# A chunked recurrence of a decoder step: turns of matrices by 64x64 products with the identity instead of 128x128 transposes

## The chip, the core and the metric

The kernel runs on one core of one Trainium2 chip. Its engines work side by side, each through its own list of instructions: TensorE (PE for its products, PEld for the loading of the stationary operand), VectorE (DVE), ScalarE (ACT), GpSimd (POOL) and SyncE (SP, which here only starts DMA transfers). They wait for each other by semaphores. The metric is the device time of one execution in microseconds (us), less is better; the median of three executions counts.

## The reference

One inference step of a two-layer decoder: an RWKV-7 time mix with a mixture of experts, then attention over a shared key/value projection with a second mixture of experts, for a prompt of 512 rows (D = 1024) and 8 single-row requests, all in fp32. The change touches only the recurrence of the time mix. Per head (16 heads of 64 features) and per row t of the prompt it is

```
def step(s, inp):
    r_t, w_t, k_t, v_t, a_t, b_t = inp
    sa = jnp.einsum('bhij,bhj->bhi', s, a_t)
    s = s * w_t[:, :, None, :] + sa[..., None] * b_t[:, :, None, :] + v_t[..., None] * k_t[:, :, None, :]
    return s, jnp.einsum('bhij,bhj->bhi', s, r_t)
s_fin, y = lax.scan(step, s0, xs)
```

with a 64x64 state s per head, started at zero for the prompt. y goes on through a norm, a gate and a projection; s_fin is an output.

## The kernel before, in words

`time_mix_chunks` cuts the 512 rows into 8 chunks of 64 and turns the scan into products. All 16 heads go together: two heads share the 128 partitions (a pair; hp says which half), and four quads of two pairs (q, p2) lie beside each other. Within a chunk the dependence of a row on earlier rows is a triangular 64x64 system per head. Its inverse is built in Tt in 5 levels, by doubling. A level (numbered l) of chunk k is a chain through four steps:

- PE turns Tt to get T (`turn_t`, 4 transposes of 128x128 through the identity, L620), and makes X from N and Tt (`solve_x`, 16 products of 64x64 with 32 columns, L606)
- DVE masks X (L766), ACT copies T out of PSUM (L841, L843)
- PE multiplies T and X (`solve_d`, 16 products, L627)
- DVE subtracts the result from Tt (L772), and the next level can start.

Two other kinds of work are laid between these steps, as fillings. The chunk behind (k-1) gets its state work: `state_v`, `state_m` (L677, L686), `turn_w` (L694), `state_u` (L704), `out_u` (L711), `add_m` (L721), one per level. The chunk ahead (k+1) is prepared: `scores_n`, `scores_b`, `scores_k` (L639, L646, L653) and the turns of V, B and K (`turn_v_b` L659 and L662, `turn_k` L668). The order is written out by hand in the loops over k and l at the end of each engine's block; nothing plans it. k runs from 0 to 8: chunk 0 has no state work beside it, chunk 7 no preparation, and k = 8 is state work alone. Ahead of the loop PE multiplies the identity with constants in `warm` (L591), results unused. POOL scales the operands of coming chunks (L910, L918). SP fills two large DRAM tables (L581, L584) at the beginning.

Of the products, 64x64 ones use one quadrant of the PE array each, by the half of the input partitions and the half of the output partitions; the list `quads` orders them so that neighbours are in other quadrants. An fp32 product stands in the trace as two LDWEIGHTS and two MATMUL records, a transpose as one of each.

Of the kernel before, what the change touches and what calls it, by code (L numbers as in the profile page):

```python
# [30 lines left out]
PAIRS = HEADS // 2  # L31
# [484 lines left out]
def time_mix_chunks(core, f, kk):  # L516
# [10 lines left out]
    with ExitStack() as own:  # L527
# [7 lines left out]
        Bt, Kt = [[by_quad(part(3, 2 * n + i, 512)) for i in range(2)] for n in range(2)]  # L535
# [3 lines left out]
        N, Tt, V, VS = tiles("N", 2, by_head), tiles("Tt", 2, by_quad), tiles("V", 3, by_quad), tiles("VS", 2, by_pair)  # L539
# [11 lines left out]
        v_ready, bt_ready, kt_ready = S("v_ready"), S("bt_ready"), S("kt_ready")  # L551
        v_copied, bt_copied, kt_copied = S("v_copied"), S("bt_copied"), S("kt_copied")
        tt0_first, tt0_new = S("first_tt0"), S("tt0_new")
        x_ready, x_masked, t_turned, t_copied, d_ready, tt_new = S("x_ready"), S("x_masked"), S("t_turned"), S("t_copied"), S("d_ready"), S("tt_new")
# [6 lines left out]
        ident = core.c("ident")  # L561
        over = lambda name, shape: core.c(name).rearrange("p (o t) -> p o t", o=1).to_broadcast([128] + shape)
# [13 lines left out]
        with nc.Block() as block:  # L576
# [11 lines left out]
            def _(pe):  # L588
                def warm(n):
                    for i in range(n):  # L590
                        pe.matmul(ps[i % 2][:, :], ident, core.const[:, 0:512], start=True, stop=True)  # L591
# [3 lines left out]
                def solve_x(k, l):  # L595
                    if l == 1:
                        pe.wait_ge(n_copied, 2 * k + 2)
                        if k:
                            pe.wait_ge(tt0_new, k)
                            pe.wait_ge(tt_new, 10 * k)  # L600
                        else:
                            pe.wait_ge(tt0_first, 1)
                    else:
                        pe.wait_ge(tt_new, 2 * (5 * k + l - 1))
                    for q, p2, hp in quads:
                        ins = pe.matmul(ps[p2][rows[hp], 32 * q:32 * q + 32], N[k % 2][rows[p2], hp, q], blocks(Tt[k % 2][rows[p2], q, hp], l, 1),  # L606
                                        start=True, stop=True)
                    ins.then_inc(x_ready, 1)

                def turn_t(k, l):  # L610
                    if l > 1:
                        pe.wait_ge(tt_new, 2 * (5 * k + l - 1))
                    elif k:
                        pe.wait_ge(tt0_new, k)
                    else:
                        pe.wait_ge(tt0_first, 1)
                    if 5 * k + l > 1:
                        pe.wait_ge(t_copied, 5 * k + l - 1)
                    for q in range(QUADS):
                        ins = pe.transpose(ps[2][:, 128 * q:128 * q + 128], Tt[k % 2][:, q], ident)  # L620
                    ins.then_inc(t_turned, 1)

                def solve_d(k, l):
                    pe.wait_ge(x_masked, 2 * (5 * k + l))
                    pe.wait_ge(t_copied, 5 * k + l)
# [4 lines left out]
                def scores_n(c):  # L630
                    if c:
                        pe.wait_ge(staged, 5 * c)
                        pe.wait_ge(kt_copied, c)
                        pe.wait_ge(bt_copied, c)
                    else:
                        pe.wait_ge(staged_first, 5)
# [19 lines left out]
                def turn_v_b(c):  # L656
                    pe.wait_ge(ks_copied, 2 * c + 2)
                    for q in range(QUADS):
                        ins = pe.transpose(ps[3][:, 128 * q:128 * q + 128], VS[c % 2][:, 2 * q:2 * q + 2], ident)  # L659
                    ins.then_inc(v_ready, 1)  # L660
                    for q in range(QUADS):
                        ins = pe.transpose(ps[4][:, 128 * q:128 * q + 128], B[c % 2][:, 2 * q:2 * q + 2], ident)  # L662
                    ins.then_inc(bt_ready, 1)

                def turn_k(c):
                    pe.wait_ge(v_copied, c + 1)
                    for q in range(QUADS):
                        ins = pe.transpose(ps[3][:, 128 * q:128 * q + 128], K[c % 2][:, 2 * q:2 * q + 2], ident)  # L668
                    ins.then_inc(kt_ready, 1)

                def state_v(c):
                    if c:
                        pe.wait_ge(m_sum, 2 * c)
                    pe.wait_ge(v_copied, c + 1)
# [6 lines left out]
                def state_m(c):  # L681
                    pe.wait_ge(vk_done, c + 1)
                    pe.wait_ge(m_new, c + 1)
                    for q, p2, hp in quads:
                        p = 2 * q + p2
                        ins = pe.matmul(wy[p2][rows[hp], :, q], M[rows[hp], p], AR[c % 4][rows[hp], p], start=False, stop=q == QUADS - 1)  # L686
                    ins.then_inc(wt_ready, 1)

                def turn_w(c):
                    pe.wait_ge(wt_copied, 2 * c + 2)  # L690
                    if c:
                        pe.wait_ge(u_copied, c)
                    for q in range(QUADS):
                        ins = pe.transpose(ps[7][:, 128 * q:128 * q + 128], WT[:, 2 * q:2 * q + 2], ident)  # L694
                    ins.then_inc(w_ready, 1)

                def state_u(c):
                    pe.wait_ge(w_copied, c + 1)
                    pe.wait_ge(tt_new, 10 * c + 10)
                    for q in range(QUADS):  # L700
                        for hp in range(2):
                            for p2 in range(2):
                                at_u = 256 * hp + 64 * q
                                ins = pe.matmul(ps[7][rows[p2], at_u:at_u + 64], Tt[c % 2][rows[p2], q, hp], W[rows[p2], q, hp], start=True, stop=True)  # L704
                    ins.then_inc(u_ready, 1)

                def out_u(c):
                    pe.wait_ge(u_copied, c + 1)
                    pe.wait_ge(y_first, 2 * c + 2)
# [4 lines left out]
                def add_m(c):  # L714
                    pe.wait_ge(y_copied, 2 * c + 2)
                    pe.wait_ge(kt_copied, c + 1)
                    for q in range(QUADS):
                        for i in range(2):
                            for p2, hp in ((0, 0), (1, 1), (0, 1), (1, 0)):
                                left, right = ((Bt[c % 2], U[rows[p2], hp, q]), (Kt[c % 2], V[c % 3][rows[p2], q, hp]))[i]  # L720
# [8 lines left out]
                scores_k(0)  # L729
                turn_v_b(0)  # L730
                for k in range(CHUNKS + 1):
                    chain, state, prep = k < CHUNKS, k >= 1, k + 1 < CHUNKS
                    for l in range(1, 6):
                        if chain:
                            turn_t(k, l)
                            solve_x(k, l)
                        if chain and l == 1:
                            turn_k(k)
# [13 lines left out]
                        if prep and l == 2:  # L752
                            scores_n(k + 1)
                        if prep and l == 3:
                            scores_b(k + 1)
                        if prep and l == 4:
                            scores_k(k + 1)
                        if prep and l == 5:
                            turn_v_b(k + 1)

            @block.vector
            def _(dve):
                def mask(k, l):
                    dve.wait_ge(x_ready, 5 * k + l)
                    for p2 in range(2):
                        dve.tensor_tensor(X[:, p2], piece(p2, 0, 32), over(f"level{l}", [QUADS, 32]), ALU.mult).then_inc(x_masked, 1)  # L766
# [33 lines left out]
                dve.tensor_copy(VS[0], f["v"][:, :, at(0)]).then_inc(staged_first, 1)  # L800
# [6 lines left out]
                for k in range(CHUNKS + 1):  # L807
                    chain, state, prep = k < CHUNKS, k >= 1, k + 1 < CHUNKS
                    for l in range(1, 6):
                        if chain:  # L810
                            mask(k, l)
                        if prep and l == 4:
                            keep_b(k + 1, 1)
                        if prep and l == 5:
                            keep_k(k + 1, 1)
                        if chain:
                            add(k, l)
                        if prep and l == 3:
                            keep_b(k + 1, 0)
                        if prep and l == 4:  # L820
                            keep_k(k + 1, 0)
                        if state and l == 4:
# [5 lines left out]
            def _(act):  # L828
                def exps(c):
                    if c == 2:  # L830
                        act.wait_ge(staged_first, 5)
                    if c > 2:
                        act.wait_ge(staged, 5 * (c - 2))
# [3 lines left out]
                def copy_t(k, l):  # L837
                    act.wait_ge(t_turned, 5 * k + l)
# [1587 lines left out]
```

## Time and profile before

| | us |
|---|---|
| median of three executions (lowest, highest) | 2183.52 (2180.32, 2188.89) |
| the profiled execution, its span | 2186.08, 2184.3 |
| chunk loop, `warm` to last state update | 295.0 to 488.8 |
| TensorE busy over the span | 1641.3 (75%) |
| mean granted clock of TensorE | 0.884 of 2.4 GHz |

The span is from the first to the last instruction of the profiled execution. The profile gives a page of sums, and the trace can be asked for stretches: busy time and counts per engine, instructions in order of time, DMA packets per queue. Times in the rows are from the start of the span. A bracket behind a row is the idle time of that engine ahead of it, with what ended it; "issue" is time in which it waited for nothing that the trace shows.

### The profile page before, as it was taken

The numbers are of one execution on the slowest core, as the hardware profiler recorded it, in microseconds if no ns is written. First come the engines' busy times: TensorE is split into PE (matmuls) and PEld (weight loads), VectorE is DVE, ScalarE is ACT, GpSimd is POOL, SyncE is SP. The second block draws the span as 40 slices with busy tenths as digits, with TensorE's granted clock in tenths as the row PEclk, the third lists the DMA queues.
The fourth block names the chain that finished last, engine by engine and source line by source line (L and its number), as shares of the span: only waits on it lengthen the run. The fifth ranks groups of instructions, "written<-read, shape, count | busy, mean of one in ns | idle before, by whom it ended". The sixth has DMA issues, their size and how long they took to land. (4 is left out here: it accounts for less than half of the span.)

```text
span 2184.3 us, 46140 instructions
## 1 busy us (share of the span) xinstructions
PE 1641.3 (75%) x20476; PEld 1226.1 (56%) x20476; DVE 627.5 (29%) x1584; ACT 374.4 (17%) x885; POOL 180.7 (8%) x166
## 2 busy tenths in 40 slices
PE   2999859981238934999980898999999526999990
PEld 2788738860225722666650676888787323666650
DVE  3100264435452152111117002000661431111117
ACT  0300323321020030111112010001660200111112
POOL 1000023410000022000004000000000120000004
PEclk7999969995578976999995998999999758999995
DMA  6020051001401136999956214442202184999953
GB/s 197 20 77 20 0 235 39 4 4 51 157 25 37 60 123 247 388 386 387 374 184 252 36 39 127 116 120 67 99 2 78 58 295 151 385 383 386 373 203 141
DMA packets 218733, 345.34 MB, mean 158 GB/s; under 512 B 69673, under 2 KB 116433, under 8 KB 218282
## 3 DMA queue, kind: packets, MB, share of 16 engines
q1 hardware_dynamic: 191354, 289.07, 37.5%
q0 software_dynamic: 9856, 33.81, 5.0%
q10 hardware_dynamic: 17328, 19.51, 2.7%
q8 instruction: 164, 2.69, 0.5%
q14 instruction: 31, 0.25, 0.0%
HBM read 295.56 MB, written 46.78 MB: 157 GB/s over the span
## 5 line engine op out<-in xcount | busy, mean ns | idle before, releaser
L1729 PE MATMUL bank<-ring_extra,xT 128*32 128x256 f32 x3456 | 194.4, 379 | 9.0 <-issue 9.0
L2123 PE MATMUL bank<-x,ring 128*128 128x256 f32 (+1 forms) x768 | 174.0, 387 | 3.4 <-issue 2.7
L426 PE MATMUL bank<-mix,ring 128*128 128x260 f32 x768 | 172.8, 386 | 4.3 <-issue 3.1
L1729 PEld LDWEIGHTS bank<-ring_extra,xT 128*32 128x32 f32 x3456 | 133.6, 110 | 65.6 <-issue 17.2
L426 PEld LDWEIGHTS bank<-mix,ring 128*128 128x128 f32 x768 | 146.1, 192 | 31.0 <-issue 8.8
L2123 PEld LDWEIGHTS bank<-x,ring 128*128 128x128 f32 x768 | 146.1, 192 | 28.1 <-issue 5.4
L1729 PE MATMUL bank<-ring,xT 128*32 128x256 f32 x2688 | 155.5, 385 | 7.5 <-issue 6.2
L1521 DVE TENSOR_TENSOR sg<-sg,bank 128x128 f32<-128x128 f32 x96 | 27.3, 285 | 377.7 <-ACT sg L1618 377.7
L1729 PEld LDWEIGHTS bank<-ring,xT 128*32 128x32 f32 x2688 | 101.7, 112 | 56.7 <-issue 15.2
L1818 PE MATMUL bank<-ring,x 128*128 128x256 f32 (+1 forms) x480 | 108.0, 386 | 2.5 <-PEq L2308 1.3
L1818 PEld LDWEIGHTS bank<-ring,x 128*128 128x128 f32 (+1 forms) x480 | 82.3, 173 | 28.3 <-issue 7.4
L1748 PE MATMUL bank<-ring_extra,hT 128*32 128x256 f32 x1728 | 97.0, 380 | 0.0
L1618 ACT ACTIVATE sg<-bank 128x128 f32<-128x128 f32 x96 | 26.7, 278 | 334.6 <-PE bank L1729 334.6
L1748 PE MATMUL bank<-ring,hT 128*32 128x256 f32 x1344 | 75.4, 380 | 0.0
L1748 PEld LDWEIGHTS bank<-ring_extra,hT 128*32 128x32 f32 x1728 | 54.9, 110 | 35.6
L1207 PE MATMUL bank<-ring,x 128*128 128x256 f32 (+1 forms) x320 | 72.1, 386 | 2.1 <-PEq L189 1.5
L1207 PE MATMUL bank<-ring,w 128*128 128x256 f32 (+1 forms) x320 | 72.1, 386 | 1.7 <-PEq L1129 1.1
L1624 ACT ACTIVATE yo<-bank 128x256 f32<-128x256 f32 x96 | 36.9, 384 | 192.9 <-PE bank L1748 192.9
L1207 PEld LDWEIGHTS bank<-ring,x 128*128 128x128 f32 (+1 forms) x320 | 55.0, 174 | 18.9 <-issue 5.0
L1207 PEld LDWEIGHTS bank<-ring,w 128*128 128x128 f32 (+1 forms) x320 | 54.9, 173 | 18.9 <-issue 4.9
L1748 PEld LDWEIGHTS bank<-ring,hT 128*32 128x32 f32 x1344 | 43.3, 110 | 27.2 <-issue 0.2
L1767 POOL DMA_DIRECT2D xe<-expert_in x32 | 16.4, 512 | 505.9 <-PE bank L1670 496.7
(364 smaller groups left out, 2177.8 us busy)
## 6 DMA issues: line engine op xcount, KB each, us to landing
ring_extra<-in_moe_w_gate SPq DMA_DIRECT2D x72, 512.0 KB, 9.5
ring_extra<-in_moe_w_up SPq DMA_DIRECT2D x72, 512.0 KB, 12.9
ring_extra<-in_moe_w_down SPq DMA_DIRECT2D x36, 1024.0 KB, 15.1
ring<-in_moe_w_gate SPq DMA_DIRECT2D x56, 512.0 KB, 9.2
ring<-in_moe_w_up SPq DMA_DIRECT2D x56, 512.0 KB, 12.6
ring<-in_moe_w_down SPq DMA_DIRECT2D x28, 1024.0 KB, 14.5
ring<-in_a_w_rkv SPq DMA_DIRECT2D x12, 1024.0 KB, 5.0
xe<-expert_in POOLq DMA_DIRECT2D x32, 384.0 KB, 8.0
```

The source lines that it names most:

```text
L426: ins = pe.matmul(ps[2 * (job % 4) + h][:, 0:HALF], w[:, kt, q * 128:(q + 1) * 128], m[:, kt, h * HALF:(h + 1) * HALF], start=kt == 0, sto ...
L1207: ins = pe.matmul(ps[job % 8][0:n, 0:256], z[:, kt, t * 128:t * 128 + n], w[:, kt, :], start=kt == 0, stop=kt == KT - 1)
L1521: dve.tensor_tensor(sg[:, u], sg[:, u], ps[i % 2][:, 0:128], ALU.mult).then_inc(gd, 1)
L1618: act.activation(sg[:, u], ps[i % 2][:, 0:128], ACT.Sigmoid).then_inc(sd, 1)
L1624: act.activation(yo[e % 2][:, u], ps[3 + i % 2][:, 0:256], ACT.Copy).then_inc(yc, 1)
L1729: ins = pe.matmul(ps[i % 2][32 * q:32 * q + 32, 0:256], xT[:, kt, 32 * u:32 * u + 32], gate_up(w[kt // 2], kt % 2, q), start=kt == 0, stop ...
L1748: ins = pe.matmul(ps[3 + i % 2][32 * r:32 * r + 32, 0:256], hT[:, u, 32 * k:32 * k + 32], w[k // 2].rearrange("p (k n) -> p k n", k=2)[:, ...
L1767: pool.dma_start(xe[e % 2][0:CAP, :], core.expert_in[CAP * e:CAP * e + CAP, :]).then_inc(xl[e % 2], 16)
L1818: ins = pe.matmul(ps[job % 6][0:n, 0:256], x[:, kt, t * 128:t * 128 + n], w[:, kt, :], start=kt == 0, stop=kt == KT - 1)
L2123: ins = pe.matmul(ps[2 * (job % 3) + h][:, 0:n], w[:, kt_, rr, :], z[:, kt_, lo:lo + n], start=kt_ == 0, stop=kt_ == 7)
```

## The change

- T, V, B, K and W are turned by 64x64 products with the identity, 16 for each matrix, where there were 4 transposes of 128x128 each. `solve_x` and `turn_t` become one function: product X and turn T alternate, 32 products, in two halves with a semaphore each, so that DVE and ACT get the first half earlier. T comes through two banks, and ACT and DVE work by halves.
- V is read from its own place; the copies to VS on DVE (L800) and POOL (L918) go. PSUM bank 7 carries T now, W and U share banks 5 and 6 with the state.
- The order of `state_m` is by pair and head half. `state_u` also waits until ACT has copied y.
- The preparation moves up a level: `scores_n` to level 1, `scores_b` to 2, `scores_k` to 3, `turn_v_b` to 4, `turn_k` to 5 (it was in level 1 of its own chunk). ACT and DVE follow.
- `warm` is called three more times: twice with 3 ahead of the loop, and once with 1 in each level of chunk 0 (its product is 128x512).

```diff
@@ PE @@
-                        pe.matmul(ps[i % 2][:, :], ident, core.const[:, 0:512], start=True, stop=True)
+                        pe.matmul(ps[5 + i % 2][:, :], ident, core.const[:, 0:512], start=True, stop=True)
...
-                def solve_x(k, l):
-                    if l == 1:
+                def solve_x_and_turn_t(k, l):
+                    if l > 1:
+                        pe.wait_ge(tt_new, 2 * (5 * k + l - 1))
...
-                    for q in range(QUADS):
-                        ins = pe.transpose(ps[2][:, 128 * q:128 * q + 128], Tt[k % 2][:, q], ident)
-                    ins.then_inc(t_turned, 1)
+                        pe.wait_ge(t_copied, 2 * (5 * k + l - 1))
+                    w = 64 if l == 1 else 32
+                    for x2 in range(2):
+                        t2 = 1 - x2
+                        right = eye[t2] if l == 1 else blocks(eye[t2], l, 0)
+                        for q in range(QUADS):
+                            for hp in range(2):
+                                x = pe.matmul(ps[x2][rows[hp], 32 * q:32 * q + 32], N[k % 2][rows[x2], hp, q], blocks(Tt[k % 2][rows[x2], q, hp], l, 1),
+                                              start=True, stop=True)
+                                t = pe.matmul(ps[t_bank[t2]][rows[1 - hp], w * q:w * q + w], Tt[k % 2][rows[t2], q, 1 - hp], right, start=True, stop=True)
+                        x.then_inc(x_ready[x2], 1)
+                        t.then_inc(t_turned[t2], 1)
...
                 def turn_v_b(c):
                     pe.wait_ge(ks_copied, 2 * c + 2)
-                    for q in range(QUADS):
-                        ins = pe.transpose(ps[3][:, 128 * q:128 * q + 128], VS[c % 2][:, 2 * q:2 * q + 2], ident)
-                    ins.then_inc(v_ready, 1)
...
+                    for src, lo in ((f["v"][:, :, at(c)], 0), (B[c % 2], 256)):
+                        for q, p2, hp in quads:
+                            ins = pe.matmul(ps[3 + hp][rows[p2], lo + 64 * q:lo + 64 * q + 64], src[rows[hp], 2 * q + p2], eye[hp], start=True, stop=True)
+                    ins.then_inc(vb_ready, 1)
...
                 def turn_w(c):
                     pe.wait_ge(wt_copied, 2 * c + 2)
...
+                    for q, p2, hp in quads:
+                        ins = pe.matmul(wy[hp][rows[p2], 0, q], WT[rows[hp], 2 * q + p2], eye[hp], start=True, stop=True)
                     ins.then_inc(w_ready, 1)
...
                 def state_u(c):
+                    pe.wait_ge(w_copied, 2 * c + 2)
+                    pe.wait_ge(y_first, 2 * c + 2)
...
                 scores_k(0)
+                warm(3)
                 turn_v_b(0)
+                warm(3)
+                turn_k(0)
                 for k in range(CHUNKS + 1):
...
                         if chain:
-                            turn_t(k, l)
-                            solve_x(k, l)
-                        if chain and l == 1:
-                            turn_k(k)
+                            solve_x_and_turn_t(k, l)
+                        if not state:
+                            warm(1)
+                        if prep and l == 1:
+                            scores_n(k + 1)
@@ ACT @@
                 def copy_t(k, l):
+                    for p2 in (1, 0):
+                        act.wait_ge(t_turned[p2], 5 * k + l)
+                        if l == 1:
+                            act.activation(T[:, p2:PAIRS:2], piece(t_bank[p2], 0, 64), ACT.Copy).then_inc(t_copied, 1)
+                        else:
+                            act.activation(blocks(T[:, p2:PAIRS:2], l, 0), packed(piece(t_bank[p2], 0, 32), l), ACT.Copy).then_inc(t_copied, 1)
@@ POOL @@
-                    pool.tensor_copy(VS[c % 2], f["v"][:, :, at(c)]).then_inc(staged, 1)
```

In the list of PE's instructions, the way into the loop (L591 is `warm`, L659, L662 and L668 the turns of V, B and K, L620 and L606 T and X of chunk 0), before:

```order
L591 MATMUL bank<-const 128x512 x3
L653 MATMUL bank<-ring 64x128 x16
L659 MATMUL bank<-const,VS_47 128x128 x4
L662 MATMUL bank<-const,ring 128x128 x4
L620 MATMUL bank<-const,Tt_42 128x128 x4
L606 MATMUL bank<-Tt_42,N_40 64x32 x16
L668 MATMUL bank<-const,ring 128x128 x4
```

and after (L594 `warm`, L658 V and B, L664 K, L616 and L618 X and T):

```order
L594 MATMUL bank<-const 128x512 x3
L651 MATMUL bank<-ring 64x128 x16
L594 MATMUL bank<-const 128x512 x3
L658 MATMUL bank<-const,v 64x64 x16
L658 MATMUL bank<-const,ring 64x64 x16
L594 MATMUL bank<-const 128x512 x3
L664 MATMUL bank<-const,ring 64x64 x16
L616 MATMUL bank<-Tt_42,N_40 64x32
L618 MATMUL bank<-const,Tt_42 64x64
```

Two blocks of `warm` came in, the turn of K moved ahead of the loop, and each turn has 16 products for 4 transposes.

On PE in level 1 of chunk 1, with the state work of chunk 0 behind it (L677 and L686), before:

```order
L620 MATMUL bank<-const,Tt_43 128x128 x4
L606 MATMUL bank<-Tt_43,N_41 64x32 x16
L668 MATMUL bank<-const,ring 128x128 x4
L627 MATMUL bank<-X,T_49 64x32 x16
L677 MATMUL bank<-ring,V_44 64x2x64 x16
L686 MATMUL bank<-ring,M_50 64x2x64 x16
L620 MATMUL bank<-const,Tt_43 128x128 x4
```

and after, from the last pairs of X and T (L616, L618) of level 1 to the first of level 2:

```order
L616 MATMUL bank<-Tt_43,N_41 64x32
L618 MATMUL bank<-const,Tt_43 64x64
L637 MATMUL bank<-ring 64x64 x16
L626 MATMUL bank<-X,T_49 64x32 x16
L673 MATMUL bank<-ring,V_44 64x2x64 x16
L682 MATMUL bank<-ring,M_50 64x2x64 x16
L616 MATMUL bank<-Tt_43,N_41 64x32
L618 MATMUL bank<-const,Tt_43 64x32
```

The two rows L616 and L618 alternate 16 times in each level; `scores_n` (L637) stands where the turn of K (L668) stood, and no 128x128 transpose is left between the 64x64 products.

## Rows read from the trace of the kernel before

**Rows 1.** The page: busy time and instructions by engine; packets of PE's instruction queue.

```profile
PE 1641.3 (75%) x20476; PEld 1226.1 (56%) x20476; DVE 627.5 (29%) x1584; ACT 374.4 (17%) x885; POOL 180.7 (8%) x166
q8 instruction: 164, 2.69, 0.5%
```

**Rows 2.** Stretches of the loop: us, busy us (instructions) per engine, PEclk, DMA share, GB/s.

```profile
320.70:334.00 13.30, 11.76 (x255) 9.91 (x248) 4.24 (x13) 2.47 (x6) 6.59 (x6) 0.51 0.90 355
376.80:396.27 19.47, 19.02 (x646) 16.32 (x645) 8.77 (x30) 7.82 (x19) 7.68 (x7) 1.00 0.02 4
337.25:457.03 119.78, 115.02 (x3866) 98.52 (x3865) 51.82 (x168) 44.90 (x105) 39.65 (x36) 1.00 0.02 4
457.03:476.90 19.87, 16.04 (x542) 13.39 (x540) 6.55 (x26) 5.90 (x14) 1.06 (x1) 1.00 0.02 4
```

**Rows 3.** PE in order of time, chunk 3: start, us, line, output<-inputs, records.

```profile
379.10 1.08 PE L677 MATMUL bank<-ring,V 64*64 64x128 f32 x32
380.27 1.96 PE L686 MATMUL bank<-ring,M 64*64 64x128 f32 x32
382.17 0.66 PE L620 MATMUL bank<-const,Tt 128*128 128x128 f32 x4
...
384.03 0.67 PE L627 MATMUL bank<-X,T 64*64 64x32 f32 x32
384.52 0.67 PE L639 MATMUL bank<-ring 64*64 64x64 f32 x32
385.31 0.66 PE L620 MATMUL bank<-const,Tt 128*128 128x128 f32 x4
```

**Rows 4.** DVE and PEld, level 2 and 3 of chunk 3; in brackets the wait ahead.

```profile
384.77 0.48 DVE L772 TENSOR_TENSOR Tt<-Tt,bank 128x128 f32<-128x128 f32 x2 [0.79 <-PE bank L627]
...
385.89 0.56 PEld L606 LDWEIGHTS bank<-Tt,N 64*64 64x64 f32 x32 [0.17 <-issue]
...
386.63 0.49 DVE L766 TENSOR_TENSOR X<-bank,const 128x128 f32<-128x128 f32 x2 [1.38 <-PE bank L606]
```

**Rows 5.** PE: warm products (L591), first turns of V (L659) and T (L620).

```profile
305.33 2.84 PE L591 MATMUL bank<-const 128*128 128x512 f32 x6
308.10 1.10 PE L646 MATMUL bank<-ring 64*64 64x128 f32 x32
...
314.42 0.66 PE L659 MATMUL bank<-const,VS 128*128 128x128 f32 x4 [1.41 <-DVE ring L780]
...
315.35 0.60 PE L620 MATMUL bank<-const,Tt 128*128 128x128 f32 x4
```

**Rows 6.** PE's weight loads, four places where it waited for "issue" amid a block.

```profile
397.22 0.20 PEld L606 LDWEIGHTS bank<-Tt,N 64*64 64x64 f32 x8 [0.22 <-issue]
...
415.87 0.14 PEld L659 LDWEIGHTS bank<-const,VS 128*128 128x128 f32 x1 [0.34 <-issue]
...
435.83 0.30 PEld L627 LDWEIGHTS bank<-X,T 64*64 64x64 f32 x10 [0.88 <-issue]
...
460.72 0.35 PEld L677 LDWEIGHTS bank<-ring,V 64*64 64x64 f32 x9 [0.77 <-issue]
```

**Rows 7.** Stretches between those four places, as in rows 2.

```profile
397.20:415.80 18.60, 17.80 (x632) 15.21 (x632) 7.98 (x27) 6.95 (x17) 7.19 (x7) 1.00 0.02 4
415.80:435.80 20.00, 18.54 (x631) 15.87 (x631) 8.23 (x27) 6.79 (x16) 7.68 (x7) 1.00 0.02 4
435.80:460.70 24.90, 23.68 (x757) 20.19 (x757) 10.81 (x36) 9.07 (x20) 3.39 (x3) 1.00 0.02 4
```

**Rows 8.** GB/s in 40 slices of 0.125 us: from 394, 412, 432 and 457 us.

```profile
GB/s 0 0 0 0 131 0 0 0 0 0 0 0 0 0 0 0 0 0 0 0 0 0 0 0 0 0 0 0 0 0 0 0 0 0 0 0 131 0 0 0
GB/s 0 0 0 0 0 0 0 0 0 0 0 0 131 0 0 0 0 0 0 0 0 0 0 0 0 0 0 0 0 0 0 0 0 0 0 0 0 0 0 0
GB/s 0 0 0 0 0 0 0 131 0 0 0 0 0 0 0 0 0 0 0 0 0 0 0 0 0 0 0 0 0 0 0 0 0 0 0 0 0 0 0 0
GB/s 0 0 0 0 0 0 0 0 0 0 131 0 0 0 0 0 0 0 0 0 0 0 0 0 0 0 0 0 0 0 0 0 0 0 0 0 0 0 0 131
```

More of the change, by code:

```diff
@@ L534, in time_mix_chunks @@
         B, K = [[by_pair(part(2, 2 * n + i, 512)) for i in range(2)] for n in range(2)]
-        Bt, Kt = [[by_quad(part(3, 2 * n + i, 512)) for i in range(2)] for n in range(2)]
+        Bt = [by_quad(part(3, i, 512)) for i in range(3)]
         BS = [by_head(part(4, i, 1024)) for i in range(2)] + [by_head(core.sb(own, "BS", [128, 1024])[:, :])]
@@ L602, in solve_x @@
                             pe.wait_ge(tt0_first, 1)
[L603 to L616, printed above, removed]
-                    if 5 * k + l > 1:
-                        pe.wait_ge(t_copied, 5 * k + l - 1)
-                    for q in range(QUADS):
-                        ins = pe.transpose(ps[2][:, 128 * q:128 * q + 128], Tt[k % 2][:, q], ident)
-                    ins.then_inc(t_turned, 1)
+                    if 5 * k + l > 1:
+                        pe.wait_ge(t_copied, 2 * (5 * k + l - 1))
[10 more added lines that the diff above has]
+                        t.then_inc(t_turned[t2], 1)
                 def solve_d(k, l):
                     pe.wait_ge(x_masked, 2 * (5 * k + l))
-                    pe.wait_ge(t_copied, 5 * k + l)
+                    pe.wait_ge(t_copied, 2 * (5 * k + l))
                     for q, p2, hp in quads:
@@ L683, in state_m @@
                     pe.wait_ge(m_new, c + 1)
-                    for q, p2, hp in quads:
-                        p = 2 * q + p2
-                        ins = pe.matmul(wy[p2][rows[hp], :, q], M[rows[hp], p], AR[c % 4][rows[hp], p], start=False, stop=q == QUADS - 1)
+                    for p in range(PAIRS):
+                        for hp in range(2):
+                            ins = pe.matmul(wy[p % 2][rows[hp], :, p // 2], M[rows[hp], p], AR[c % 4][rows[hp], p], start=False, stop=p // 2 == QUADS - 1)
                     ins.then_inc(wt_ready, 1)
@@ L690, in turn_w @@
                     pe.wait_ge(wt_copied, 2 * c + 2)
[L691 to L694, printed above, removed]
+                    for q, p2, hp in quads:
+                        ins = pe.matmul(wy[hp][rows[p2], 0, q], WT[rows[hp], 2 * q + p2], eye[hp], start=True, stop=True)
                     ins.then_inc(w_ready, 1)
                 def state_u(c):
-                    pe.wait_ge(w_copied, c + 1)
+                    pe.wait_ge(w_copied, 2 * c + 2)
+                    pe.wait_ge(y_first, 2 * c + 2)
                     pe.wait_ge(tt_new, 10 * c + 10)
@@ L809, in _ @@
                     for l in range(1, 6):
[L810 to L817, printed above, removed]
                         if prep and l == 3:
@@ L821, in _ @@
                             keep_k(k + 1, 0)
+                        if chain:
+                            mask(k, l)
+                        if prep and l == 3:
+                            keep_b(k + 1, 1)
+                        if prep and l == 4:
+                            keep_k(k + 1, 1)
+                        if chain:
+                            add(k, l)
                         if state and l == 4:
@@ L872, in copy_w @@
                     act.wait_ge(w_ready, c + 1)
-                    act.activation(W, by_quad(ps[7][:, :]), ACT.Copy).then_inc(w_copied, 1)
+                    for hp in range(2):
+                        act.activation(W[:, :, hp], wy[hp][:, 0], ACT.Copy).then_inc(w_copied, 1)
                 def copy_u(c):
                     act.wait_ge(u_ready, c + 1)
-                    act.activation(U, by_head(ps[7][:, :]), ACT.Copy).then_inc(u_copied, 1)
+                    for hp in range(2):
+                        act.activation(U[:, hp], wy[hp][:, 0], ACT.Copy).then_inc(u_copied, 1)
                 exps(0)
```

84 lines of the change are left out of this document (39 added, 45 removed).

## The prediction, made before the changed kernel was run

> **What bounds the kernel now.** I read the page first, then the stretches of the chunk loop, then PE's instructions one by one, and last the packets of PE's instruction queue. The page shows PE as the busiest engine and a queue of its own for instructions: 164 packets, 2.69 MB, so 16.4 KB each [rows 1]. PE ran 2 x 20476 loads and products, 250 to a packet.
>
> The chunk loop is the only place that changes. Chunk 3 takes 19.47 us, with PE busy for 19.02 and PEld for 16.32, DVE for 8.77 and ACT for 7.82; chunks 1 to 6 take 119.78 us together, 19.96 each, at a clock of 1.00. Chunk 7 takes 19.87, and the stretch from 320.7 to 334 in chunk 0 ran at a clock of 0.51, the lower level of 1.2 GHz [rows 2]. So at first sight PE bounds the loop, with the chain of each level (T, X, mask, D, subtraction) close behind.
>
> There is a second bound, and I give it the most weight. At four places PE waits for "issue" amid a block whose operands are all there, 0.22 to 0.88 us [rows 6]. Between them lie 632, 631 and 757 products, each with its load: 1264, 1262 and 1514 instructions, which is 5, 5 and 6 times 252.5 [rows 7]. So the waits sit on the borders of PE's instruction packets (the few missing to a full packet are waits that are instructions of their own). Ahead of each a packet of 131 GB/s starts: at 394.5, 413.5, 432.9 and 458.3 us [rows 8], and PE goes on 2.7, 2.4, 2.9 and 2.5 us later [rows 6], 2.6 on the mean. After two of these the window shows the next packet too, at 398.5 and 461.9, 1.3 and 1.2 us after PE went on [rows 6, 8]. I read this so: the next packet is asked for only once PE has entered the last one, and a packet therefore lasts at least 1.25 + 2.6 = 3.85 us (ends of the parts: 3.6 and 4.2). A chunk before has 2 x 644 instructions, 5.1 packets, 19.6 us by this; it touches the limit at its dense places and loses some 0.5 us a chunk.
>
> The Trainium skill says in Advanced Engine Details and Errata, ISA Cache, that the instruction cache has lines of 16 KB or 256 instructions, "Only 2 cache lines!", and also that TensorE's is 128 KB. The trace agrees on the packet (16.4 KB) and looks like two lines. By the 128 KB there would be more lines ahead and no such limit; that would give the first rival's time.
>
> **The change part by part, first without that limit.** The costs of PE: 16 products over four quadrants with up to 64 columns take 0.46 to 0.49 us (384.03 to 384.52), four transposes 0.58 (385.31 to 385.89), in which 0.17 goes to the change of array mode that PEld's bracket shows; `state_m` 1.90 with that change behind it, 1.73 without, in two quadrants with 128 columns; `state_v` 1.17 to the start of the next [rows 3, 4]. From `state_m` I take 0.87 for 128 columns in four quadrants (`scores_b`, `scores_k`) and for 64 columns in two (`state_u`), and twice 0.46 for `add_m` with its 32 products. From the end of a block's issue to DVE's start it is 0.28 us (384.03 + 0.46 to 384.77), and a pair of DVE steps takes 0.48 [rows 3, 4].
>
> - X and T: before 0.58 + 0.46 = 1.04, now 32 products, 0.92. X's first half is ready at 0.46 + 0.28, so the first mask hides under the second half; the second runs from 1.20 to 1.49. D starts at 1.54 of the level where it was 1.04 + 0.28 + 0.49 + 0.05 = 1.86. With D 0.46, 0.28, 0.48 and 0.06 a bare level falls from 3.14 (382.17 to 385.31 in rows 3) to 2.82.
> - Level 1: D at 1.64 (T's copies have all 64 columns), D to 2.10, `state_v` 1.17, `state_m` 1.73: 5.00, before 5.37. Level 2: D to 2.00, `scores_b` 0.87: 2.87, before 3.14. Levels 3 to 5, before 10.96 (385.31 to 396.27): level 3 has 0.92, `state_u`, D and `scores_k`, 3.15; level 4 waits for the masked scores until 2.16 and turns V and B, 3.08; level 5 has 0.92, `add_m`, D, then 0.82 to the next level, 3.13. Sum 17.2, before 19.47; I say 17.3 [rows 2, 3].
> - ACT makes pairs of half copies where it made one whole copy, less than 0.1 us each and 5 to 6 of them a chunk, under PE: nothing. The copies to VS go from POOL, which is idle more than half of the chunk [rows 2]: nothing. Should the cover be gone, ACT's would be 0.5 us a chunk.
> - `state_u` waits for the copy of y too. Beside a chunk this ends about when PE gets there. At the end, k = 8, where nothing covers it, it costs 0.55, and the halves 0.15: +0.7 us.
> - `state_m` in another order: neighbours still lie in two quadrants, so 1.73 stays. Nothing either way.
> - The start: three `warm` products take 2.77 us (305.33 to 308.10 in rows 5), so two blocks add 5.5 and the turn of K 0.5, of which 1.3 falls into the 1.41 that PE waited for the masks; the loop starts at 320.05, not 315.35 [rows 5]. In chunk 0 a `warm` of 1.07 stands in each level: levels of 3.9, 3.5, 3.5, 3.5 and 3.4, 17.9 in all; before it was 21.9, with the low clock in it. By rows 2 the clock fell after a thinly filled stretch; the `warm` products fill it, and I count full clock. With 0.3 for packets chunk 0 ends at 338.2, before 337.25: +1.
>
> On the turns the Trainium skill speaks against the change: TensorE: Matmul & The Clock Gate, Terms, calls the transpose mode 4x faster for fp32. Taken per array that would make each turn some 1.7 us, and nine turns a chunk 10 us more. The rows do not show it: 64x64 products use four quadrants at once, and 16 of them pass in 0.46 us.
>
> **The limit on instructions.** A turn by products is 64 instructions for 8 (16 products of two loads and two products, for 4 transposes of one each). Nine turns a chunk: 9 x 56 = 504 more, 1288 + 504 = 1792, or 7.10 packets. They would have to pass in 17.3 us, 2.4 us each, where the rows allow 3.85. So a chunk takes 7.10 x 3.85 = 27.3 us (25.6 and 29.8 at the ends 3.6 and 4.2), and all that was gained above is covered by waits for instructions.
>
> - Chunks 1 to 6: 6 x (27.3 - 19.96) = +44.2 (33.6 to 59.1).
> - Chunk 7: 1408 instructions, 5.58 packets, 21.5 us; before 19.87: +1.6 (0.2 to 3.6).
> - Start and chunk 0: from the end of `scores_k` 1580 instructions, 6.26 packets, 24.1 us, about the 25.0 of the work itself. But the fills keep the DMA engines at 0.90 until 334 [rows 2], and packets wait behind them: +4. The ends are +1 (the sum above) and +8 (1.5 more and half of the 13.3 us at the low clock, should it come again).
> - k = 8: +0.7.
>
> Sum +50.5 (35.5 to 71.4). The profiled execution took 2186.1 us for a span of 2184.3; it becomes 2236.6, and as it lies 2.6 above the median of the runs, I say 2234 us. By the ends 2219 and 2255.
>
> **Rivals.** First: no such limit; the four waits are something else, or more packets can be under way once PE asks for them faster. For it: in chunks 1 to 6, 7731 instructions and so 30.6 packets in 119.78 us [rows 2], only a few of the borders show a long wait. Against it: they pass at 3.9 us each, just what the limit allows, and the distances fit multiples of one packet three times. Then it is the sum without the limit: a chunk of 17.3 + 0.6 = 17.9, 6 x -2.06 = -12.4, chunk 7 -1.8 (18.1 for 19.87), +1 and +0.7: -12.5, 2171 us. It decides as soon as a packet can come in 2.4 us. This is the one on the faster side.
>
> Second: the limit holds, but it is shorter when PE stands still, as the request may go out at once; at 3.0 us a packet a chunk takes 21.3, +8.0 for six, with the start and the end +10: 2194 us. Against it: the four waits were such standstills and still had 1.25 + 2.6.
>
> Third: the waits for instructions bring TensorE to its lower clock. Then PE's issue of 15.9 us a chunk becomes 31.9: 6 x 11.9 = 71.6, chunk 7 +4.6, start +9: 2270 us. For it: in chunk 0 the clock fell to 0.51. Against it: chunk 7 had 540 loads in 19.87 us at 1.00 [rows 2], 27 per us; the chunks would have 896 in 27.3, 33 per us.
>
> **Numbers.** The forecast has 0.80, the first rival 0.09, the second 0.06, the third 0.05. The range is from 2208 to 2255: the ends of the packet's time, and some of the way to the second rival. It leaves out the first rival and most of the other two. A difference of 0.5% (11 us) is about what can be told from none: faster 0.09, within it 0.02, slower 0.89.
>
> **What would show it.** Right: PE waits for "issue" at nearly every 250th instruction of the loop, for 1 us and more, packets of its instruction queue come every 3.6 to 4.2 us through the whole loop, and six chunks take some 164 us; DVE and ACT wait for PE throughout. The bare chain of a level is still seen at 1.54 from X to D wherever no border falls in it. Wrong: packets closer than 3.4 us, or a chunk under 22 us. If chunk 0 shows the low clock, the `warm` products did not do what I count; if rows at 1.2 GHz run through chunks 1 to 6, it is the third rival.

## The result, and the profile after

The kernel after takes 2255.27 us (median of 4; 2252.0 to 2260.48), the kernel before 2182.83 (median of 4): a ratio of 1.033, 95% interval 1.0301 to 1.0359, so it is slower. The profiled execution took 2256.0 us for a span of 2254.2, before 2186.08 for 2184.3 [rows 1 and the table]. The span grew by 69.9 us.

The page after: PE's busy time and the packets of its instruction queue, 180 where there were 164 [rows 1].

```profile
PE 1665.4 (74%) x22514; PEld 1247.4 (55%) x22514; DVE 629.5 (28%) x1583; ACT 383.9 (17%) x965; POOL 176.7 (8%) x159
q8 instruction: 180, 2.95, 0.6%
```

Stretches of the kernel after, columns as in rows 2: chunk 0, chunks 1 to 6, chunk 2 alone, chunk 7, k = 8. A chunk goes from ACT's first copy of T to that of the next; the last ends with POOL's M.

```profile
323.31:347.31 24.00, 19.47 (x696) 14.13 (x692) 7.83 (x25) 6.34 (x22) 6.02 (x5) 0.93 0.56 220
347.31:511.45 164.14, 116.71 (x5379) 108.64 (x5372) 54.35 (x169) 51.58 (x165) 37.57 (x32) 0.95 0.02 5
376.07:403.29 27.22, 18.37 (x910) 17.06 (x906) 9.07 (x29) 8.97 (x28) 7.11 (x7) 1.00 0.02 5
511.45:536.16 24.71, 18.60 (x701) 16.86 (x695) 6.64 (x24) 5.41 (x18) 1.39 (x2) 0.82 0.02 4
536.16:547.68 11.52, 5.68 (x195) 4.93 (x192) 1.51 (x4) 2.53 (x8) 1.06 (x1) 0.99 0.01 1
```

Before, cut in the same way:

```profile
315.99:337.88 21.89, 18.48 (x456) 15.32 (x456) 7.45 (x24) 5.51 (x12) 6.59 (x6) 0.69 0.77 301
337.88:457.67 119.79, 115.03 (x3872) 98.53 (x3872) 52.17 (x168) 44.91 (x105) 39.86 (x37) 1.00 0.02 4
457.67:478.01 20.34, 16.49 (x568) 13.78 (x568) 6.20 (x24) 5.54 (x13) 1.91 (x2) 1.00 0.02 4
478.01:488.76 10.75, 5.64 (x167) 4.76 (x164) 1.51 (x4) 2.40 (x6) 1.05 (x1) 0.97 0.01 3
```

Chunks 1 to 6 take 164.14 us for 119.79, 27.36 each. PE is busy for 116.71 us of them, before for 115.03: nearly all of the loss is time in which PE stands still. What it waited for, PE over chunks 1 to 6 (us in total, times, longest), after:

```profile
PE bank L626 <- issue: 12.2, 9, 1.9
PE bank L616 <- issue: 7.1, 4, 1.9
PE bank L704 <- issue: 5.0, 4, 1.5
...
PE bank L616 <- DVE Tt L769: 1.9, 6, 0.3
PE bank L698 <- issue: 1.6, 2, 1.1
```

and before:

```profile
PE bank L721 <- DVE w L786: 1.4, 5, 0.3
PE bank L627 <- issue: 0.8, 1, 0.8
PE bank L659 <- issue: 0.2, 1, 0.2
```

Over all rows of this view the waits for "issue" are 45.0 us in 34 after (27 of them 1 us and longer), 1.0 us in 2 before. They lie in every kind of block (D, X, T, scores, turns), so it is not an operand that is late. Where they lie shows in the loads of chunk 2 (columns as in rows 6):

```profile
385.61 0.30 PEld L644 LDWEIGHTS bank<-ring 64*64 64x64 f32 x10 [1.21 <-issue]
...
389.62 0.26 PEld L626 LDWEIGHTS bank<-X,T 64*64 64x64 f32 x11 [1.36 <-issue]
...
393.52 0.26 PEld L704 LDWEIGHTS bank<-ring,U 64*64 64x64 f32 x11 [1.51 <-issue]
...
397.51 0.13 PEld L616 LDWEIGHTS bank<-Tt,N 64*64 64x64 f32 x1 [2.04 <-issue]
...
401.27 0.32 PEld L626 LDWEIGHTS bank<-X,T 64*64 64x64 f32 x16 [1.81 <-issue]
```

They come 4.0, 3.9, 4.0 and 3.8 us apart. GB/s in slices of 0.1 us from 384, 388 and 392 us, as in rows 8:

```profile
GB/s 0 0 0 0 0 0 0 0 0 0 0 0 0 0 0 0 0 0 0 0 0 0 0 0 0 0 0 164 0 0 0 0 0 0 0 0 0 0 0 0
GB/s 0 0 0 0 0 0 0 0 0 0 0 0 0 0 0 0 0 0 0 0 0 0 0 0 0 0 164 0 0 0 0 0 0 0 0 0 0 0 0 0
GB/s 0 0 0 0 0 0 0 0 0 0 0 0 0 0 0 0 0 0 0 0 0 0 0 0 0 0 0 164 0 0 0 0 0 0 0 0 0 0 0 0
```

The only traffic is a packet at 386.7, 390.6 and 394.7 us. Each starts 1.0 to 1.2 us after PE went on, and PE goes on again 2.8 to 2.9 us later: the cycle that rows 6 and 8 showed at four places now stands at nearly every border. Between two waits lie 253 and 255 instructions, 126 products and 127 loads, then 128 and 127:

```profile
385.50:389.60 4.10, 2.76 (x126) 2.65 (x127) 1.78 (x4) 2.06 (x6) 1.27 (x1) 1.00 0.02 4
389.60:393.40 3.80, 2.53 (x128) 2.39 (x127) 2.26 (x6) 0.75 (x3) 0.00 (x0) 1.00 0.02 4
```

PE passes them in 2.76 and 2.53 us of busy time and stands for the rest. So it is not that each instruction takes too long to issue: the time is lost at the borders. Over chunks 1 to 6 there are 43 packets, 3.87 us apart on the mean (3.3 to 4.6); before 30, 3.92 apart.

Behind the loop the span lost 11.0 us more: 11.5 lost in the gate of the time mix, whose products (L1183, before L1182) are the same. After and before:

```profile
744.62 0.70 PE L1184 MATMUL bank<-v,k 32*128 32x260 f32 x2
...
747.39 1.24 PE L1183 MATMUL bank<-v,k 128*128 128x260 f32 x2
```

```profile
698.65 0.70 PE L1183 MATMUL bank<-v,k 32*128 32x260 f32 x2
```

A product takes 1.16 us (747.39 to the next at 748.55) where it took 0.63 (698.65 to 699.28). The stretches of the granted clock there, after, then before:

```profile
746.50:771.00 24.50, 24.23 (x42) 10.21 (x42) 4.06 (x11) 0.00 (x0) 0.00 (x0) 0.50 0.00 0
```

```profile
684.00:703.00 19.00, 17.89 (x57) 8.28 (x57) 6.12 (x16) 0.00 (x0) 0.00 (x0) 1.00 0.00 0
```

It is the lower level, 1.2 GHz, while PE was busy without a gap; ahead of the fall at 745.5 us it had been busy at 2.4 GHz since 738.9, as before.

The 69.9 us, in order: 3.5 ahead of the loop (where nothing changed; in the ten other profiles the loop starts between 293.7 and 299.6 us), 3.8 for its start, 2.1 in chunk 0, 44.35 in chunks 1 to 6, 4.4 in chunk 7, 0.8 in k = 8, 11.0 behind.

### The profile page after: what moved, and what is told of

It is laid out like the page before. It is cut to its first block and busy times, and to the rows that moved or that the text cites. A ratio compares the mean times of both kernels' runs of the same rounds, so it can differ in the third digit from the quotient of the medians.

```text
span 2254.2 us, 50273 instructions
## 1 busy us (share of the span) xinstructions
PE 1665.4 (74%) x22514; PEld 1247.4 (55%) x22514; DVE 629.5 (28%) x1583; ACT 383.9 (17%) x965; POOL 176.7 (8%) x159
## 5 line engine op out<-in xcount | busy, mean ns | idle before, releaser
L1730 PEld LDWEIGHTS bank<-ring_extra,xT 128*32 128x32 f32 x3456 | 133.5, 110 | 65.8 <-issue 17.3
L1522 DVE TENSOR_TENSOR sg<-sg,bank 128x128 f32<-128x128 f32 x96 | 27.3, 285 | 377.8 <-ACT sg L1619 377.8
L1819 PEld LDWEIGHTS bank<-ring,x 128*128 128x128 f32 (+1 forms) x480 | 82.1, 173 | 28.3 <-issue 7.5
L616 PE MATMUL bank<-Tt,N 64*64 64x32 f32 x1280 | 52.4, 224 | 13.3 <-issue 9.0
```

The lines of the kernel that those rows point to most:

```text
L616: x = pe.matmul(ps[x2][rows[hp], 32 * q:32 * q + 32], N[k % 2][rows[x2], hp, q], blocks(Tt[k % 2][rows[x2], q, hp], l, 1), start=True, sto ...
L1522: dve.tensor_tensor(sg[:, u], sg[:, u], ps[i % 2][:, 0:128], ALU.mult).then_inc(gd, 1)
L1730: ins = pe.matmul(ps[i % 2][32 * q:32 * q + 32, 0:256], xT[:, kt, 32 * u:32 * u + 32], gate_up(w[kt // 2], kt % 2, q), start=kt == 0, stop ...
L1819: ins = pe.matmul(ps[job % 6][0:n, 0:256], x[:, kt, t * 128:t * 128 + n], w[:, kt, :], start=kt == 0, stop=kt == KT - 1)
```

## Experiments

The ratios are to executions of the kernel before that were timed beside each group: 2189.31 us for the first four kernels below, 2187.9 for the halved ones and those about `warm`, 2187.31 for pad_quads. Loads and products a chunk are counted from the rows: 1288 before, 1792 after.

**Only the order and the warm products (order_only).** The kernel after with all turns made by 128x128 transposes again (and the copies to VS back); K's turn stands for all.

```diff
-                    for q, p2, hp in quads:
-                        ins = pe.matmul(ps[3 + hp][rows[p2], 64 * q:64 * q + 64], K[c % 2][rows[hp], 2 * q + p2], eye[hp], start=True, stop=True)
+                    for q in range(QUADS):
+                        ins = pe.transpose(ps[3][:, 128 * q:128 * q + 128], K[c % 2][:, 2 * q:2 * q + 2], ident)
```

> The changed kernel with every turn (T, V, B, K, W) made by 128x128 transposes again, on banks 2, 3, 4 and 7 as before, and the copies to VS back; the new order of the fillings, the new warm products and the order of state_m stay. Theory (instruction supply): 1288 loads and products a chunk as before, so packets need 5.1 x 3.85 = 19.6 us; chunks 1 to 6 take 19.0 to 19.9 us each and the time is 2176 to 2184 us, within 0.4% of before. Rival (the order and the warm products are what costs): it stays near the changed kernel, 2240 us and more, with chunks of 25 us and more.

Measured 2189.65 us, ratio 1.0018 (0.9996 to 1.0039). Chunks 1 to 6:

```profile
342.48:461.39 118.91, 112.21 (x3876) 97.91 (x3872) 52.55 (x168) 43.67 (x106) 39.41 (x36) 1.00 0.02 5
```

The time was to be 2176 to 2184 us and is a little above; against its own base it lies within the 0.4% expected. So the order with the warm products costs at most 0.4%, and the loss hangs on the turns by products, with the halves and banks that came with them.

**Four of the nine turns (t_transposes).** After, with the five turns of T by transposes, those of V, B, K and W by products: 1512 loads and products a chunk.

```diff
-                                t = pe.matmul(ps[t_bank[t2]][rows[1 - hp], w * q:w * q + w], Tt[k % 2][rows[t2], q, 1 - hp], right, start=True, stop=True)
...
+                    for q in range(QUADS):
+                        ins = pe.transpose(ps[2][:, 128 * q:128 * q + 128], Tt[k % 2][:, q], ident)
```

> The changed kernel with T alone turned by 128x128 transposes again (5 of the 9 turns of a chunk); V, B, K and W by 64x64 products. Theory: 1792 - 5 x 56 = 1512 loads and products, 5.99 packets, 22.5 to 23.5 us a chunk, so about 4.2 us x 7 less than the changed kernel: 2224 to 2230 us. Rival (the split into halves, or the products themselves, are slow, not the supply): all of the loss comes from X and T, so it falls to that of before, 2185 us; or none of it does and it stays at 2255.

Measured 2218.94 us, ratio 1.0132 (1.008 to 1.0185).

```profile
340.27:477.68 137.41, 120.22 (x4544) 104.42 (x4545) 52.63 (x168) 45.95 (x136) 37.87 (x32) 0.96 0.02 5
```

22.90 us a chunk, as expected (22.5 to 23.5); 1512 / 252.5 x 3.87 is 23.2. The whole time came out under the 2224 to 2230 us that I expected, although 10.2 us of its loss lie behind the loop. What counts here is the chunk: its loss grows with the number of instructions.

**Instructions without the turns, first try (pad_many, pad_few).** The kernel before with useless products ahead of T in each level: 16 with 32 columns, or 2 with 256.

```diff
@@ pad_many @@
+                    for i in range(8):
+                        for h in range(2):
+                            pe.matmul(ps[2][rows[h], 32 * i:32 * i + 32], ident[rows[h], 64 * h:64 * h + 64], core.const[rows[h], 0:32], start=True, stop=True)
@@ pad_few @@
+                    for h in range(2):
+                        pe.matmul(ps[2][rows[h], 0:256], ident[rows[h], 64 * h:64 * h + 64], core.const[rows[h], 0:256], start=True, stop=True)
```

> The kernel before, with 16 extra products of 64x64 by 32 columns ahead of the turn of T in each level of chunks 0 to 7 (results unused, two quadrants, 64 loads and products, about 0.43 us of PE). Theory: 1608 loads and products a chunk, 6.37 packets, 24 to 25 us a chunk; with chunks 0 and 7 +33 to +40 us: 2216 to 2223 us, and waits for issue at nearly every border. Rival (PE's time is the bound, not the number of instructions): the same as pad_few, at most 5 x 0.43 = 2.2 us a chunk, +17 us: 2200 us.

> The kernel before, with 2 extra products of 64x64 by 256 columns at the same place (8 loads and products, the same 0.43 us of PE, the same two quadrants). Theory: 1328 loads and products, 5.26 packets = 20.2 us, below what the work itself then takes, 19.5 + 2.2 = 21.7 us a chunk: +15 to +18 us, 2198 to 2201 us, with few waits for issue. Rival (PE's time bounds): the same time, and then pad_many has it too; the two kernels differ only where the number of instructions counts.

Measured 2222.54 us, ratio 1.015 (1.0107 to 1.0193), and 2201.85, ratio 1.0075 (1.0049 to 1.01). The first time is as expected and the second 0.85 us above its range, and yet the pair settles nothing. One sign failed: pad_many was to wait at nearly every border. PE in pad_many and in pad_few:

```profile
405.67 1.07 PE L621 MATMUL bank<-const 64*64 64x32 f32 x32
406.67 0.66 PE L623 MATMUL bank<-const,Tt 128*128 128x128 f32 x4
```

```profile
388.91 0.60 PE L620 MATMUL bank<-const 64*64 64x256 f32 x4
389.44 0.66 PE L622 MATMUL bank<-const,Tt 128*128 128x128 f32 x4
```

The 16 products take 1.00 us to the start of the next block, the 2 take 0.53. The PE time is not equal, as I had meant: the 16 stand in two quadrants. That is 2.35 us a chunk, nearly all of the 2.85 between the two (24.62 and 21.77), and waits for "issue" are only 2.5 us in six chunks of pad_many.

**The same with four quadrants (pad_quads).**

```diff
+                    for n in range(4):
+                        for i, o in ((0, 0), (1, 1), (0, 1), (1, 0)):
+                            pe.matmul(ps[i][rows[o], 384 + 32 * n:416 + 32 * n], ident[rows[i], 64 * i:64 * i + 64], core.const[rows[i], 0:32], start=True, stop=True)
```

> The kernel before with 16 added products of 64x64 with 32 columns ahead of X in each level, results unused, spread over all four quadrants as X is (my earlier 16 stood in two quadrants and took 1.0 us a level, so that they cost PE time as well as instructions). By X's own block they take 0.46 us of PE, less than the 0.53 of the two wide products that brought a chunk to 21.8 us. If PE's time decides, a chunk takes 19.96 + 5 x 0.35 to 0.46 = 21.7 to 22.3 us with hardly a wait for issue, ratio 1.007 to 1.009. If packets of instructions decide, 1608 loads and products are 6.37 packets of 3.87 us, 24.6 us a chunk; PE's busy time over six chunks stays near 130 us and waits for issue take some 15: ratio 1.014 to 1.017.

Measured 2216.37 us, ratio 1.0137 (1.0067 to 1.0207). One block, the six chunks, and the two longest of PE's waits in them:

```profile
403.55 0.67 PE L607 MATMUL bank<-const 64*64 64x32 f32 x32
404.04 0.65 PE L609 MATMUL bank<-Tt,N 64*64 64x32 f32 x32
```

```profile
343.26:491.33 148.07, 135.94 (x4832) 117.99 (x4832) 52.70 (x168) 44.88 (x104) 40.65 (x37) 0.96 0.02 4
```

```profile
PE bank L630 <- issue: 4.0, 4, 1.6
PE bank L609 <- issue: 1.8, 4, 0.5
```

The block takes 0.49 us, less than that of pad_few, and a chunk 24.68 us against 21.77. The packets decide: 1608 / 252.5 x 3.87 is 24.6, and packets came 3.87 us apart. The waits for "issue" are 10.3 us, not 15, since PE's busy time rose to 135.9 and not to 130. Over the six chunks the kernel lost 28.3 us: the 30 blocks of 0.49 us are 14.7, the waits 10.3, and 6.8 us at the lower clock (441.0 to 447.8 us) can have cost at most 3.4. In pad_few 30 blocks of 0.53 us cost only 10.8 us, so pad_quads lost 17.5 more with shorter blocks, and the clock can explain a fifth of that.

**Half the products in both kernels (after_half, before_half).** Each product takes the moving columns of two quads, the stationary operand of the first: 896 and 680 loads and products a chunk. These kernels leave out the stationary operands of every second quad, and the decay (its exponents are scaled by 0). Their outputs are not those of the reference and the parts behind the loop work on other data, so only the loop counts.

```diff
-                quads = [(q, p2, hp) for q in range(QUADS) for p2, hp in ((0, 0), (1, 1), (0, 1), (1, 0))]
+                quads = [(q, p2, hp) for q in range(0, QUADS, 2) for p2, hp in ((0, 0), (1, 1), (0, 1), (1, 0))]
...
-                        ins = pe.matmul(ps[hp][rows[p2], 256 + 32 * q:288 + 32 * q], T[rows[hp], 2 * q + p2], X[rows[hp], p2, q], start=True, stop=True)
+                        ins = pe.matmul(ps[hp][rows[p2], 256 + 32 * q:320 + 32 * q], T[rows[hp], 2 * q + p2], X[rows[hp], p2, q:q + 2], start=True, stop=True)
```

> The kernel after with half the products in the chunk loop, each with twice the columns (every product takes the moving columns of two neighbouring quads, its stationary operand from the first alone), so 896 loads and products a chunk where there were 1792; the same columns pass. What it leaves out: the second quad's own stationary operands, and the decay (exponents are scaled by 0, so that values stay bounded). Routing further on has other data, so only the chunk loop counts. Limit on instructions: 896 are 3.55 packets, 13.7 us, no longer more than the chain needs. The chain was 17.3 without the limit; X with T falls from 0.92 to some 0.5, D from 0.46 to 0.25 (16 small products are bound by their number, not their columns), five times: 17.3 - 3.2 = 14.1; I expect 14 to 15.5 us a chunk, against 27.4, and waits at packet borders small. Rival (turns by products, or the new chain of semaphores, are slow in themselves; the packets only happen to fit): the chunk stays above 20 us, and above the kernel before with the same halving.

> The kernel before with half the 64x64 products in the chunk loop, each with twice the columns, transposes as they were: 680 loads and products a chunk for 1288, 2.7 packets. It leaves out the same things as the halved kernel after. Its chain without a limit: 19.47 less 0.42 a level (X and D 0.46 to 0.25 each), 17.4; I expect 16.8 to 17.8 us a chunk for 19.96. So by the limit on instructions the order of the two kernels turns round: halved, after is some 3 us a chunk faster than before (14.1 to 17.4), where in full it is 7.4 slower. Rival (turns slow in themselves): halved before stays faster than halved after.

One execution of each: 2194.1 and 2162.22 us. Chunks 1 to 6, after_half and before_half:

```profile
336.44:431.85 95.41, 87.91 (x2698) 69.35 (x2689) 52.34 (x169) 48.89 (x165) 37.01 (x32) 1.00 0.02 4
```

```profile
330.42:435.94 105.52, 98.84 (x2044) 70.67 (x2048) 52.04 (x168) 43.63 (x105) 39.64 (x37) 1.00 0.03 9
```

15.90 and 17.59 us a chunk, with no wait for "issue" in either. The order of the two kernels turns round: with few instructions the kernel after is 1.7 us a chunk faster (3 expected), in full 7.4 slower. So neither the turns by products nor the new chain are slow in themselves. I had counted 14.1 for after_half, and 15.90 lies above the whole range of 14 to 15.5; before_half, counted at 17.4, lies in its range. The new chain is longer than I count it. From the first product of X and T to the first of D it takes 1.39 to 1.83 us in after_half. In the full kernel after, in the second level of chunk 4, where no border falls in it, it takes 1.78:

```profile
434.41 0.24 PE L616 MATMUL bank<-Tt,N 64*64 64x32 f32 x1
...
436.19 0.67 PE L626 MATMUL bank<-X,T 64*64 64x32 f32 x32
```

**The warm products (warm_only, after_no_warm).** Before with the added `warm` calls alone, and after without them.

```diff
                 scores_k(0)
+                warm(3)
                 turn_v_b(0)
+                warm(3)
...
+                        if not state:
+                            warm(1)
```

> The kernel before with the added warm products alone (two blocks of 3 ahead of the loop, 1 in each level of chunk 0). My count: the blocks put the loop's first T 4.1 us later (5.5 less the 1.4 that PE waited anyway); chunk 0 falls from 21.9 to 18.7 us, since the 13.7 us at a clock of 0.5 in it go. Sum +0.9 on the loop's end: ratio 1.000, at most 0.3% either way. Rival: the warm products do not hold the clock and cost their 5.5 + 5.3 us: ratio 1.004 to 1.005, chunk 0 above 22 us.

> The kernel after without the added warm products. Start 4 us earlier; chunk 0 has 1560 loads and products, 6.2 packets, 24 us whether warm or not, if the clock stays up; with a stretch at the lower clock, as before the change, up to 27. So the end of the loop moves by -4 to 0 us: ratio to before 1.031 to 1.034. Rival: the starved loop falls to the lower clock for longer once nothing fills chunk 0: more than 5 us of it at 0.5, ratio 1.035 or above.

Measured 2194.87 us, ratio 1.0022 (0.9998 to 1.0047), and 2245.65, ratio 1.0243 (1.0196 to 1.029). Chunk 0 in warm_only, in order_only (which has them too) and in after_no_warm:

```profile
322.04:343.22 21.18, 18.56 (x466) 12.80 (x467) 7.45 (x24) 5.52 (x13) 6.59 (x6) 1.00 0.67 261
```

```profile
323.82:342.48 18.66, 18.05 (x470) 12.61 (x466) 7.44 (x24) 5.30 (x13) 6.60 (x6) 1.00 0.73 285
```

```profile
317.35:341.60 24.25, 18.23 (x685) 17.23 (x681) 7.91 (x25) 6.45 (x20) 6.04 (x5) 0.71 0.59 230
```

They do hold the clock in chunk 0 (1.00 for 0.69 before, 0.93 for 0.71 in the kernels after), but in warm_only chunk 0 took 21.18 us, not the 18.7 that I expected from order_only: it waited 1.5 us for "issue" amid `scores_k`, while the fills were still running. In the kernel after, from the loop's first instruction to the last M, the time with them is 4.2 us longer (249.2 for 245.1), just over the most that I had allowed. But the difference does not lie where they stand. Chunks 1 to 6, which have none of them, without the warm products ahead:

```profile
341.60:498.58 156.98, 117.79 (x5385) 110.64 (x5382) 54.72 (x169) 51.44 (x164) 37.49 (x32) 0.93 0.02 5
```

That is 26.16 us a chunk for 27.36 with the same instructions: 42 packets, 3.69 us apart for 3.87. Chunk 7 and k = 8 took 40.2 us for 36.2, start and chunk 0 47.9 for 48.8. So a packet's time is not one fixed number, and why it differs between these two kernels is open. The ratio without the warm products is lower than the 1.031 to 1.034 that I said, and its interval lies below that of the kernel after, but 4.8 us of the difference between the profiles lie ahead of the loop, where the two are equal; how much the warm products cost in full is open. No kernel that computes the whole step beats the kernel before.

## Why the prediction was right, step by step

- **The time as a whole: at the very end of its range.** Said 2234 us (2208 to 2255), measured 2255.27, so 0.27 above the upper number as it is written and 21 above the forecast. Slower was right and the largest term was right; the excess comes from chunk 7 and from terms outside the loop (below).
- **The limit on instructions, the step with the most weight: right.** Said 7.10 packets of 3.85 us, 27.3 us a chunk; measured 27.36, packets 3.87 us apart. Shown by three things that agree: four of nine turns gave 22.90, products that turn nothing gave 24.68, and halving the instructions took the waits away and turned the sign. What was only argued is the mechanism, that a packet is asked for once PE has entered the last. The rows fit it: at the 34 waits of chunks 1 to 6 PE went on 2.2 to 2.9 us after a packet's start (2.6 on the mean), and the next packet started 1.0 to 1.9 us after that (1.3). In before_half, where PE never waited, packets came only 6.5 us apart, one for 255 loads and products, so they follow what PE uses. No run changed how far ahead they are asked for.
- **Its signs.** Waits at nearly every border, of 1 us and more: seen, 27 of 34. Packets every 3.6 to 4.2 us: 31 of 42 intervals; one, 3.32 us, is under the 3.4 that was to speak against it. The bare chain of 1.54 us from X to D: not seen. In level 2 of the six chunks, where no border fell and only the turn of W stands between, it took 1.77 to 1.96.
- **Chunks 1 to 6:** +44.2 said, +44.35 measured. That they agree so closely is in part luck: the time of a packet was read from four waits, with ends that gave 33.6 to 59.1, and the same instructions without the warm products took 156.98 us, +37.2.
- **Chunk 7:** +1.6 (0.2 to 3.6) said, +4.4 measured, a term mis-sized. The instruction count does not explain it; the row of chunk 7 has a clock of 0.82, with 10.2 us at the lower level from 510.0 us on. Of the eleven kernels, chunks 1 to 6 have stretches at the lower clock in the four whose waits for "issue" there come to 10 us and more (after, after_no_warm, t_transposes, pad_quads), and in none of the seven with 4 us or less. So part of the third rival came true: the clock fell in the starved loop, for short stretches in chunks 1 to 6 (their clock is 0.95) and again in chunk 7, which the prediction counted at full clock. That the waits for packets covered it there and not in chunk 7 is my reading; it was not tried.
- **Start and chunk 0:** +4 (1 to 8) said, +5.9 measured (3.8 and 2.1). The warm products held the clock in chunk 0 nearly (0.93); the packets behind the fills took the rest. (The five levels listed for chunk 0 add up to 17.8 us, not 17.9, which changes nothing.)
- **k = 8:** +0.7 said, +0.8 measured.
- **The gain without the limit:** said 2.1 us a chunk; halved kernels showed 1.7. The full chain at 17.3 was not seen and stays open; with a step from X to D of 1.77 and more for the 1.54 counted it is likely longer.
- **What no term had:** 3.5 us ahead of the loop and 11.0 behind it, both put at nothing. The sum over the loop was 50.5 for 55.5 measured; with these two the span's 69.9. Without them the time would have been some 2241 us, well inside the range.
- **The lower clock in the gate of the time mix** stood for 30.7 us in all four kernels that turn V, B, K and W by products (after, t_transposes, after_no_warm, after_half), at the most 13.7 us in the seven others. It goes with the change, then, but the products there and ahead of it are the same and PE was as busy. After_half never waited for packets in chunks 1 to 6 and has it too, so the starved loop is not its cause. The cause is open.
- **Rivals:** no limit (2171 us, 17.9 a chunk) is refuted by the run itself and by pad_quads; 3.0 us a packet (2194) by the spacing, of which none in the six chunks was under 3.3; the low clock through the loop (2270) came only in short stretches.

## What to carry to other kernels

Count loads and products (an fp32 product is four instructions, a transpose two) and divide by the time that they are to pass in. Here PE was supplied with 65 to 68 instructions per us over a long stretch (252.5 in 3.87 us, in after_no_warm in 3.69). In this kernel, where the blocks were busy for less than that time, shorter blocks did not help; only fewer instructions took the waits away, by wider products or by the transposes. Look for waits for "issue" that recur every 250 loads and products: they name this bound, although PE's busy share (71% of chunks 1 to 6) and every semaphore point elsewhere.

## What was not expected of the hardware

- Sixteen 64x64 products with 32 columns take 1.00 us in two quadrants and 0.49 us in four; two products with 256 columns, eight times as wide, take 0.53. At 32 columns the number of products in each quadrant set the time, not their columns: 8 in each of two quadrants took twice as long as 4 in each of four.
- While the DMA engines were at 0.90 and more with the fills, the packets of PE's instruction queue came 5.2 to 7.7 us apart in the kernel after (they start at 318.5, 326.2, 331.4 and 336.6 us); with the fills done, 3.4 to 3.7 us apart (340.0, 343.7, 347.4). PE waited 1.8 us for "issue" up to 328.6.
- TensorE fell to 1.2 GHz for 30.7 us in the middle of densely filled products, in four of eleven kernels, and that cost 11.5 us in the kernel after. A stretch of the same length stands later in all eleven (778.3 to 809.0 us before, 847.9 to 878.6 after).
